# A hybrid mixer and MoE layer on one core: six 256-column slots of the first projection as seven block products each, with the convolution's channels among them

## The chip, the cores and the metric

The kernel is one program on one core of a Trainium2 chip. The metric is device time in microseconds, the median over runs. Engines: PE (TensorE, matmul), with its weight loads shown as PEld, DVE (VectorE), ACT (ScalarE), POOL (GpSimd), and SP (SyncE), which here only issues DMAs. All arithmetic on PE is float32: the profile shows every float32 matmul as two MATMUL records, so 16 records of 512 columns are 8 matmuls.

## The reference, cut to what matters

```python
h = layer_norm(x, ln_in_g, ln_in_b)                 # (1024 tokens, 1024 channels)
proj = h @ w_in                                     # 7432 columns
(a_q, a_k, a_v, b_q, b_f, b_i, b_g, c_z, c_xbc, c_dt,
 d_q, d_k, d_v, d_f, gate) = split(proj)            # 512 128 128 256 256 256 256 256 512 4
                                                    # 256 256 256 4 4096
ya = swa_sink_attention(a_q, a_k, a_v, ...)         # mixer A
yb = hgrn2_mixer(b_q, b_f, b_i, b_g, ...)           # mixer B, the linear mixer: forget gate
                                                    # f = lb + (1-lb)*sigmoid(b_f), then log, cumsum
yc = mamba2_mixer(c_z, c_xbc, c_dt, ...)            # mixer C, convolution over c_xbc
yd = forgetting_attention(d_q, d_k, d_v, d_f)       # mixer D
g = sigmoid(gate)
merged = g0*(ya@w_br_a) + g1*(yb@w_br_b) + g2*(yc@w_br_c) + g3*(yd@w_br_d)
h = layer_norm(ALPHA*h + merged @ w_out)
h = layer_norm(ALPHA*h + moe_ffn(h))                # 64 experts, top 6, and a shared one
```

## The kernel before, in words

The input projection is cut into slots: 256 columns of w_in (1 MB), loaded by SP into one of two SBUF buffers (`g.wslot`, slot n into buffer n % 2). load_slot(n) waits until PE has used slot n-2. A slot has units. A feature-major unit ("fm", L284) makes 128 channels for 512 tokens: 8 matmuls of 512 columns over the 1024 input channels. A token-major unit ("tm", L290) makes 256 channels for 2 x 128 tokens: 16 matmuls of 256 columns (136 for the slot of mixer A's values and the eight small row channels). Units alternate between PSUM banks 6 and 7; ACT copies each out with one or two activations (read_unit, L303).

Stage 1 (norm_in_and_project) loads and normalizes x, turns it with PE transposes into `g.hT` (channels on partitions) in two halves of 512 tokens, and projects slots 0 to 7: two of mixer A's queries, BF (forget gate), AK, the AV slot with the small rows, BQ, and BI and BG (mixer B's values and gates, tm). PE's own order is: transposes of the first half, units 0 and 1, transposes of the second half (L619), unit 2, a small table of biases (bias_rows, L628), then all the other units. Beside it POOL writes the rows of h to DRAM (L470, L472, DMA L474, eight times: the h_rows loop). ACT and DVE make the forget gate: Sigmoid (L522) once BF is out, scale (L585), key and floor (L589, L591), Ln (L528), two scans (L595).

Then one block holds mixers A, B, C and D, one after another on every engine. Each mixer's PE code calls fill(n) between its own steps, which issues n parts (an eighth of a unit) of the following slots: in mixer A those of CX (c_xbc, 512 channels in two slots, fm, destination `g.cX`), in B those of CZ, DQ, DK, DV and a gate slot, in C three gate slots. A gate unit is staged by ACT (L328) in one buffer that a DMA of SP spills to DRAM (L355) before the next may be staged.

In mixer D eleven gate slots are computed in the block form: the product of the weight slot (2 x 2 blocks of 512 input channels x 128 output channels) with hT (2 x 2 blocks of 512 x 512) is made from seven block products of 4 matmuls each (gate_part, L1566), instead of 32 matmuls. It needs four sums of hT's blocks (t1 to t4, DVE, L1649 to L1654), four sums of weight blocks in every slot (mix_weights, POOL, L1517 to L1522), and combinations of results: ACT copies products r = 0, 2, 4, 6 out of one bank (L1731), DVE adds or copies r = 1, 3, 5 from the other (L1670, L1666), POOL adds two of the results (L1539). A product is allowed when the one two before it has left its bank. In D's start PE waits for all units of mixer C to be read out (`pe.wait_ge(g.proj_read, g.first_unit[g.slots_d])`), does fill(8), that is products r = 0 and 1, and then waits for a row that comes by way of DVE (`drop`, L1656), SP's DMAs (L1495) and the semaphore drop_in, before its first scores (L1595).

After the mixers come the merge, output projection with routing, and the experts (L2840, L2856), whose weights (3 MB each) SP streams when PE has finished with a buffer.

## Time and profile before

| | us |
|---|---|
| median of 3 runs (2185.29 to 2189.09) | 2185.38 |
| the profiled execution, its own time | 2187.7 |
| its span, first to last instruction | 2185.9 |
| PE busy | 2091.0 (96%) |
| DVE, POOL, ACT busy | 1058.4, 666.8, 423.2 |
| mean granted TensorE clock | 0.985 |

Busy times of two engines overlap. Matmul durations of the profile contain the pipeline's length, so what a matmul costs in a stream is read from the distance of starts. The granted clock is 1.00 at 2.4 GHz and 0.50 at 1.2 GHz.

### The profile page before, as it was taken

Reading aid. Unit: us, or ns where it says so; the run is one execution under the profiler, and the core shown is the slowest. Engines: PE = TensorE matmul, PEld = TensorE weight load, DVE = VectorE, ACT = ScalarE, POOL = GpSimd, SP = SyncE. Lnnn points to the kernel's source line nnn. Section 1 sums busy time; section 2 is a strip of 40 time slices with the busy share of each in tenths; the row PEclk is TensorE's granted clock in tenths of the full one; section 3 lists DMA queues with packets and bytes.
Section 4 is the critical chain, followed back from the end, with each engine's and each line's share of the span. In section 5 each row is a group of like instructions: output and inputs, shape, how many; then the busy total and the mean of one; then the engine's idle time right before and its main releaser. Section 6 shows DMA issues by size and latency. Waiting matters only on the chain. (4 is left out here: it accounts for less than half of the span.)

```text
span 2185.9 us, 23006 instructions
## 1 busy us (share of the span) xinstructions
PE 2091.0 (96%) x7177; PEld 1102.2 (50%) x7178; DVE 1058.4 (48%) x2940; ACT 423.2 (19%) x909; POOL 666.8 (31%) x582
## 2 busy tenths in 40 slices
PE   7999999999999999999999999899999999999990
PEld 4458667574644455553444554344444444444440
DVE  4010455558561222221223755686666666666646
ACT  2020333334321111111221222011111111111112
POOL 0800002221132212112442001355545545555533
PEclk9999999999999999999999999999999999999995
DMA  5311001002122211116336004699999999999964
GB/s 144 131 49 39 20 20 32 27 20 68 44 68 77 77 54 62 54 63 226 106 96 222 34 35 163 229 336 348 350 353 359 358 360 354 350 349 355 350 200 155
DMA packets 129900, 368.24 MB, mean 168 GB/s; under 512 B 34332, under 2 KB 66192, under 8 KB 104352
## 3 DMA queue, kind: packets, MB, share of 16 engines
q1 hardware_dynamic: 104224, 312.64, 38.4%
q0 software_dynamic: 23520, 54.61, 10.4%
q8 instruction: 44, 0.72, 0.1%
q10 hardware_dynamic: 2080, 0.01, 0.1%
q14 instruction: 32, 0.26, 0.0%
HBM read 318.37 MB, written 68.16 MB: 177 GB/s over the span
## 5 line engine op out<-in xcount | busy, mean ns | idle before, releaser
L2840 PE MATMUL banks<-arena 128*128 128x512 f32 x1056 | 468.8, 597 | 3.0 <-DVE arena L2833 0.8
L284 PE MATMUL banks<-arena 128*128 128x512 f32 x864 | 397.3, 596 | 3.0 <-PEq L108 3.0
L2819 POOL DMA_INDIRECT arena<-h_rows,index x268 | 276.4, 1031 | 153.3 <-DVE index L2803 73.9
L2840 PEld LDWEIGHTS banks<-arena 128*128 128x128 f32 x1056 | 195.2, 190 | 225.8 <-issue 224.7
L1566 PE MATMUL banks<-arena 128*128 128x512 f32 x616 | 282.7, 601 | 3.1 <-ACT arena L328 3.1
L2856 PE MATMUL banks<-arena 128*128 128x512 f32 x528 | 237.6, 592 | 1.3 <-ACT arena L2655 0.8
L284 PEld LDWEIGHTS banks<-arena 128*128 128x128 f32 x864 | 157.7, 192 | 154.7 <-issue 144.7
L2833 DVE STREAM_TRANSPOSE arena<-arena 128x1024 f32<-128x1024 f32 x66 | 133.9, 2028 | 133.5 <-PE banks L2840 133.5
L2827 POOL DMA_INDIRECT sums<-arena,row_to x66 | 107.1, 1623 | 274.4 <-DMA sums<-arena,row_to 250.4
L1566 PEld LDWEIGHTS banks<-arena 128*128 128x128 f32 x616 | 111.6, 192 | 120.8 <-issue 115.8
L2856 PEld LDWEIGHTS banks<-arena 128*128 128x128 f32 x528 | 100.2, 190 | 127.0 <-issue 125.3
L2803 DVE TENSOR_SCALAR index<-row 32x1 uint32<-32x1 f32 x1072 | 155.4, 145 | 17.1
L1815 PE MATMUL banks<-arena 128*128 128x512 f32 x320 | 138.1, 593 | 1.6 <-DMA arena<-in_w_br_d_dram 1.6
L290 PE MATMUL banks<-arena 128*128 128x256 f32 (+1 forms) x640 | 129.6, 360 | 0.0
L1977 PE MATMUL banks<-arena 128*128 128x512 f32 x256 | 114.2, 600 | 4.2 <-PEq L1785 2.8
L290 PEld LDWEIGHTS banks<-arena 128*128 128x128 f32 x640 | 110.9, 190 | 13.5 <-issue 1.4
L2650 ACT ACTIVATE arena<-banks 128x256 f32<-128x256 f32 x65 | 24.9, 383 | 434.6 <-PE banks L2840 434.6
L1844 DVE TENSOR_TENSOR arena<-arena,banks 128x512 f32<-128x512 f32 x64 | 44.0, 688 | 129.9 <-PE banks L1815 98.6
L1815 PEld LDWEIGHTS banks<-arena 128*128 128x128 f32 x320 | 60.4, 190 | 78.9 <-issue 68.9
L793 DVE CUSTOM_DVE_ANT_0 arena<-banks,arena,sinks 128x192 f32<-128x192 f32 (+1 forms) x64 | 23.6, 406 | 127.9 <-PE banks L735 71.0
L2565 DVE TENSOR_SCALAR arena<-banks,weight 128x512 f32<-128x512 f32 x64 | 48.0, 750 | 75.7 <-PE banks L2856 75.7
L2662 ACT ACTIVATE arena<-banks,weight 128x512 f32<-128x512 f32 x64 | 44.0, 687 | 203.6 <-PE banks L2856 203.6
(376 smaller groups left out, 2254.3 us busy)
## 6 DMA issues: line engine op xcount, KB each, us to landing
arena<-in_w_exp_gate_dram SPq DMA_DIRECT2D x66, 1024.0 KB, 8.8
arena<-in_w_exp_up_dram SPq DMA_DIRECT2D x66, 1024.0 KB, 11.5
arena<-in_w_exp_down_dram SPq DMA_DIRECT2D x66, 1024.0 KB, 18.1
arena<-in_w_in_dram SPq DMA_DIRECT2D x26, 1024.0 KB, 5.3
gates<-arena SPq DMA_DIRECT2D x60, 256.0 KB, 2.0
arena<-gates SPq DMA_DIRECT2D x60, 256.0 KB, 2.6
arena<-h_rows,index POOLq DMA_INDIRECT x268, 3.0
arena<-in_x_dram SPq DMA_DIRECT2D x8, 512.0 KB, 5.9
```

What stands on the lines that cost most here:

```text
L284: mm = pe.matmul(bank[0:width], w[:, q, col:col + width], g.hT[:, q, at * HALF:(at + 1) * HALF], start=(q == 0), stop=(q == KT - 1))
L290: mm = pe.matmul(bank[:, m * width:(m + 1) * width], g.hT[:, k, (at + m) * P:(at + m + 1) * P], w[:, k, col:col + width], start=(k == 0), ...
L1566: mm = pe.matmul(gate_bank(n, b), left[:, k, :], right[:, k, :], start=(alone and k == 0), stop=(k == 3), skip_group_check=True)
L1815: mm = pe.matmul(bank[:, 4 + p % 2, :], wbr[:, k, j * P:(j + 1) * P], g.yT[:, k, h * HALF:(h + 1) * HALF], start=(k == tiles[b][0]), stop= ...
L1977: mm = pe.matmul(bank[:, h, :], merged[:, k, m * P:(m + 1) * P], wout[k][:, h * HALF:(h + 1) * HALF], start=(k == 0), stop=(k == KT - 1))
L2565: dve.tensor_scalar(w.y[c % 2][:, HALF:], bank[:, 5, :], g.weight[:, c % 4:c % 4 + 1], None, ALU.mult).then_inc(s["yb"], 1)
L2803: ins = dve.tensor_scalar(g.index[32 * b:32 * b + 32, k, q:q + 1], g.row[32 * q:32 * q + 32, k, :], 4.0, float(b), ALU.mult, ALU.add)
L2819: return pool.indirect_dma_start(w.x[k][:, 256 * q:256 * (q + 1)], None, rows, bass.IndirectOffsetOnAxis(ap=g.index[:, k, q:q + 1], axis=0 ...
L2827: return pool.indirect_dma_start(g.sums, bass.IndirectOffsetOnAxis(ap=g.row_to[:, b:b + 1], axis=0), w.y[k], None, bounds_check=last, oob_ ...
L2833: return dve.transpose(w.xT.rearrange("p k (q n) -> p q k n", q=4), w.x[k].rearrange("p (q n k) -> p q k n", q=4, k=KT))
L2840: mm = pe.matmul(g.bank[:, 2, :].rearrange("p (a f) -> p a f", a=2), xT[:, k, :], wgu[:, :, k, :], start=(k == 0), stop=(k == KT - 1))
L2856: mm = pe.matmul(g.bank[:, 4 + h, :], hidT[:, k, :], wdn[:, k, h * HALF:(h + 1) * HALF], start=(k == 0), stop=(k == 1))
```

## The change

Six slots of stage 1 (BF, the two of mixer A's queries, BQ, and both CX) are made in the block form, 28 matmuls instead of 32, with results written straight to their destinations. Their products use the same banks 6 and 7, and the same split over ACT, DVE and POOL. Slots 0 and 1 are now AK (one piece) and AV with the small rows (three pieces); their six units come first in the order key, value, value, key, value, value, so that three units precede the transposes of the second half. BI and BG leave stage 1 and become the fill of mixer A in place of CX. The sums t1 to t4 are made on DVE after the second half of hT is there, t3 a second time later into another place. POOL gets the weight sums and the crossing adds between its h_rows steps. Semaphores of the block form are shared with mixer D, whose counts start at six slots. D's first product waits for one unit fewer, its second for the last.

```diff
+    keys = [(0, unit) for unit in fm(halves(g.kA, HD))]
+    values = [(1, unit) for unit in tm(values_and_rows, 0, P + 8, 2)]
+    slot([(0, AK, P)], [keys[0], values[0], values[1], keys[1]])
+    slot([(0, AV, P), (P, CDT, 4), (P + 4, DF, 4)], values[2:])
+    g.rows_unit = sum(len(x.units) for x in S)
+    g.blocks_from = len(S)
+    slot(whole(BF), [])            # and two of AQ, BQ, two of CX: no units
...
+    g.slots_a = len(S)
     slot(whole(BI), tm(wide(g.igB, 0), 0, 256, 2))
     slot(whole(BG), tm(wide(g.igB, 256), 0, 256, 2))
-    g.slots_a = len(S)
-    for c in range(2):
-        slot(whole(CX + 256 * c), fm(...cX...) + fm(...cX..., P))
     g.slots_b = len(S)
@@ SP, stage 1
             load_slot(g, sp, 0)
+            load_slot(g, sp, 1)
             (x tiles 4 to 7, small parameters)
-            load_slot(g, sp, 1)
+            load_slot(g, sp, 2)
...
-            for n in range(2, g.slots_a + 2):
+            for n in range(3, g.slots_a + 2):
+                if 0 <= n - 2 - g.blocks_from < N:
+                    sp.wait_ge(prod, 7 * (n - 1 - g.blocks_from))
                 load_slot(g, sp, n)
@@ POOL, stage 1
+            def mix_weights(n):            # four tensor_tensor of 128x512, as in mixer D
+            def cross(n):
+                pool.wait_ge(copied, 4 * n + 3)
+                pool.wait_ge(joined, 3 * n + 2)
+                pool.tensor_tensor(kept(n, 4), kept(n, 4), kept(n, 3), ALU.add).then_inc(crossed, 1)
+            mix_weights(0)
+            mix_weights(1)
+            keep_row(0); keep_row(1); cross(0); keep_row(2); keep_row(3); mix_weights(2)
+            keep_row(4); cross(1); keep_row(5); keep_row(6); mix_weights(3); keep_row(7)
+            cross(2); mix_weights(4); (clears); cross(3); mix_weights(5); ...; cross(4); cross(5)
@@ ACT, stage 1
+            for n in range(N):
+                for r in range(0, 7, 2):
+                    act.wait_ge(prod, 7 * n + r + 1)
+                    if r == 6:
+                        act.wait_ge(crossed, n + 1)
+                    act.activation(kept(n, r), block_bank(n, 0), ACT.Copy).then_inc(copied, 1)
+                    (n == 3, r == 0: Ln)
+                (n == 0: Sigmoid, when copied >= 4, joined >= 3, crossed >= 1)
@@ DVE, stage 1
+            t1, t3, t2, t4 after turned(1)
+            join(0); forget gate scale; rows copy; join(1); join(2); key; floor; t3_late
+            join(3); scans; join(4); join(5)
@@ PE, stage 1
+            def block_part(n, r):          # 4 matmuls of 128x512
+                if r == 0: waits for the slot's load and joined >= 3n
+                elif r == 1: copied >= 4n
+                elif r % 2: joined >= 3n + r // 2
+                else: copied >= 4n + r // 2
+                if r == 2: wsum >= 4n + 4, tsum >= 4 (5 from n = 4)
@@ PE, mixer D
-                if n:
-                    pe.wait_ge(s["joined"], 3 * n)
+                pe.wait_ge(*((s["joined"], 3 * (first + n)) if n else (g.proj_read, g.first_unit[g.slots_d] - 1)))
             elif r == 1:
-                if n:
-                    pe.wait_ge(s["copied"], 4 * n)
+                pe.wait_ge(*((s["copied"], 4 * (first + n)) if n else (g.proj_read, g.first_unit[g.slots_d])))
...
-        pe.wait_ge(g.proj_read, g.first_unit[g.slots_d])
         fill(8, "start")
```

## Rows read from the trace of the kernel before

**Rows 1.** Stages: time, busy PE, PEld, DVE, ACT, POOL (instructions), granted clock, DMA share, GB/s.

```profile
47.15:222.75 175.60, 175.58 (x633) 110.12 (x632) 10.34 (x11) 24.61 (x39) 45.43 (x30) 0.99 0.23 77
222.75:344.70 121.95, 120.19 (x593) 79.31 (x594) 57.72 (x224) 41.11 (x153) 3.78 (x2) 1.00 0.08 27
...
1460.00:2080.00 620.00, 615.94 (x1901) 291.75 (x1900) 406.85 (x1401) 75.24 (x168) 312.87 (x276) 1.00 1.00 354
```

**Rows 2.** SP's waits over the whole span: total us, times, longest.

```profile
SPq L2353 <- PE banks L2856: 585.3, 61, 17.3
```

**Rows 3.** PE in order of time, stage 1: start us, us, what.

```profile
32.66 3.66 PE L619 MATMUL banks<-ident,arena 128*128 128x128 f32 x32
...
43.12 4.11 PE L628 MATMUL banks<-arena 32*128 32x256 f32 x16
47.16 77.15 PE L284 MATMUL banks<-arena 128*128 128x512 f32 x176
124.14 14.99 PE L290 MATMUL banks<-arena 128*128 128x136 f32 x128
...
167.31 55.42 PE L290 MATMUL banks<-arena 128*128 128x256 f32 x256
```

**Rows 4.** Groups of mixer D's block form: busy us, mean ns, idle before.

```profile
L1731 ACT ACTIVATE arena<-banks 128x512 f32<-128x512 f32 x44 | 26.2, 595 | 139.8 <-PE banks L1566 137.4 <-DMA gates<-arena 2.4
...
L1670 DVE TENSOR_TENSOR arena<-arena,banks 128x512 f32<-128x512 f32 x22 | 15.1, 686 | 48.9 <-PE banks L1566 48.9
L1520 POOL TENSOR_TENSOR arena<-arena 128x512 f32<-128x512 f32 x11 | 14.1, 1283 | 0.0
```

**Rows 5.** Mixer B, steps of L1075 with tm fill between, then with fm fill.

```profile
356.87 1.47 PE L1075 MATMUL banks<-arena 128*16 128x32 f32 x16
...
366.20 1.47 PE L1075 MATMUL banks<-arena 128*16 128x32 f32 x16
...
384.85 1.47 PE L1075 MATMUL banks<-arena 128*16 128x32 f32 x16
...
394.15 1.47 PE L1075 MATMUL banks<-arena 128*16 128x32 f32 x16
```

**Rows 6.** POOL in order of time: two consecutive h_rows transfers.

```profile
70.25 0.58 POOL L474 DMA_DIRECT2D h_rows<-arena  x1 [0.31 <-POOL arena L472]
...
75.93 0.57 POOL L474 DMA_DIRECT2D h_rows<-arena  x1 [0.30 <-POOL arena L472]
```

**Rows 7.** ACT in order of time: the forget gate's Sigmoid.

```profile
111.22 1.28 ACT L522 ACT_TABLE_LOAD   x1
112.52 1.91 ACT L522 ACTIVATE arena<-arena 128x2048 f32<-128x2048 f32 x1
```

**Rows 8.** DVE in order of time: statistics of x tiles 4 to 7.

```profile
20.53 4.83 DVE L537 BATCH_NORM_STATS2 stats<-arena 128x6 f32<-128x512 f32 x8
```

**Rows 9.** The stretch in which the AV slot's three pieces are loaded (columns as in rows 1).

```profile
111.80:115.00 3.20, 3.20 (x9) 1.42 (x8) 0.00 (x0) 2.61 (x2) 0.00 (x0) 1.00 0.96 169
```

**Rows 10.** All engines in order of time where mixer D starts.

```profile
634.35 0.60 ACT L328 ACTIVATE arena<-banks 128x512 f32<-128x512 f32 x1
...
637.77 10.12 PE L1566 MATMUL banks<-arena 128*128 128x512 f32 x16 [3.12 <-ACT arena L328]
...
646.78 1.26 POOL L1517 TENSOR_TENSOR arena<-arena 128x512 f32<-128x512 f32 x1 [2.11 <-DMA arena<-arena]
...
647.73 0.39 PE L1595 MATMUL banks<-arena 128*128 128x128 f32 x2
```

**Rows 11.** Three stretches and their granted clock (columns as in rows 1).

```profile
46.50:49.90 3.40, 3.40 (x6) 1.21 (x6) 0.00 (x0) 0.79 (x2) 0.00 (x0) 0.50 0.37 154
...
637.77:643.80 6.03, 6.03 (x7) 2.52 (x8) 5.16 (x2) 0.00 (x0) 5.86 (x4) 0.50 0.70 217
...
990.11:993.13 3.02, 0.00 (x0) 0.03 (x1) 0.00 (x0) 0.78 (x2) 0.00 (x0) 1.00 0.24 90
```

More of the change, by code:

```diff
@@ L390, in norm_in_and_project, with weights, sums, block_bank @@
     ones_rows = g.region(YT0 + 8192, T)
+    N = len(g.block_out)
+    half = slice(0, 4), slice(4, 8)
+    tok = [[g.hT[:, k, h * HALF:(h + 1) * HALF] for h in range(2)] for k in half]
+    t1, t2 = g.region(R2 + 4096, 4, HALF), g.region(R2 + 6144, 4, HALF)
+    t3, t4 = g.region(R3 + 2056, 4, HALF), g.region(R3 + 4 * (T + 3), 4, HALF)
+    t3_late = g.region(YT0, 4, HALF)
+    mixed = [[g.region(a, 4, P) for a in at] for at in (
+        (R3, R3 + 512, R3 + 1024), (R3 + 1536, WK + 4608, R1 + 7296),
+        (YT0 + 2048, YT0 + 2560, YT0 + 3072), (YT0 + 3584, YT0 + 4096, YT0 + 4608))]
+    g.block_sems = {n: sem("k_" + n) for n in "tsum wsum prod copied joined crossed".split()}
+    tsum, wsum, prod, copied, joined, crossed = (g.block_sems[n] for n in "tsum wsum prod copied joined crossed".split())
+    def weights(n):
+        w = g.wslot[(g.blocks_from + n) % 2]
+        return [[w[:, k, i * P:(i + 1) * P] for k in half] for i in range(2)]
+    def sums(n):
+        return mixed[n % 2 if n < 4 else 2 + n % 2]
+    def block_bank(n, b):
+        return bank[:, 6 + (n + b) % 2, :]
+    def kept(n, r):
+        a, b = g.block_out[n]
+        place = {0: (a, 0), 1: (a, 0), 2: (a, 1), 5: (a, 1), 4: (b, 1), 3: (b, 0), 6: (b, 0)}[r]
+        return place[0][:, place[1] * HALF:(place[1] + 1) * HALF]
+    def loaded(eng, n):
+        eng.wait_ge(g.w_loaded[(g.blocks_from + n) % 2], slot_bytes(g, g.blocks_from + n))
     def row(a):
@@ L466, in _, with keep_row @@
             pool.wait_ge(rel_ready, 4)
-            for m in range(NT):
+            def keep_row(m):
                 if m >= 2:
@@ L474, in _ @@
                 pool.dma_start(g.h_rows[m * P:(m + 1) * P, :], h_row[m % 2]).then_inc(h_kept[m % 2], 16)
+            keep_row(0)
+            keep_row(1)
+            cross(0)
+            keep_row(2)
+            keep_row(3)
+            mix_weights(2)
+            keep_row(4)
+            cross(1)
+            keep_row(5)
+            keep_row(6)
+            mix_weights(3)
+            keep_row(7)
+            cross(2)
+            mix_weights(4)
             for k in range(2):
@@ L479, in _ @@
             pool.memset(ones_rows[:, 0:T:P], 0.0).then_inc(cleared, 1)
+            cross(3)
+            mix_weights(5)
             for b in range(2):
@@ L586, in _ @@
                                   ALU.mult, ALU.add).then_inc(gate, 1)
+            dve.wait_ge(rows_turned, 1)
+            dve.tensor_copy(g.rows[:].rearrange("p (b n) -> p b n", b=2), bank[0:8, 0:2, :]).then_inc(rows_read, 1)
+            join(1)
+            join(2)
             dve.wait_ge(gate, 2)
@@ L596, in _ @@
                                        ALU.mult, ALU.add).then_inc(scanned, 1)
+            for n in range(4, N):
+                join(n)
             dve.wait_ge(scanned, 2)
-            dve.wait_ge(rows_turned, 1)
-            dve.tensor_copy(g.rows[:].rearrange("p (b n) -> p b n", b=2), bank[0:8, 0:2, :]).then_inc(rows_read, 1)
             dve.wait_ge(rows_read, 1)
@@ L633, in _ @@
             pe.wait_ge(g.const_ready, 4)
+            def block_part(n, r):
+                (a11, a12), (a21, a22) = weights(n)
+                s1, s2, s4 = sums(n)
+                third = t3 if n < 4 else t3_late
+                left, right, b, alone = ((a11, tok[0][0], 0, True), (a12, tok[1][0], 1, True), (s2, t2, 0, False),
+                                         (s1, t1, 1, True), (a21, third, 0, False), (s4, tok[1][1], 1, False),
+                                         (a22, t4, 0, False))[r]
+                if r == 0:
+                    loaded(pe, n)
+                    pe.wait_ge(*((joined, 3 * n) if n else (g.proj_read, g.rows_unit - 1)))
+                elif r == 1:
+                    pe.wait_ge(*((copied, 4 * n) if n else (g.proj_read, g.rows_unit)))
+                elif r % 2:
+                    pe.wait_ge(joined, 3 * n + r // 2)
+                else:
+                    pe.wait_ge(copied, 4 * n + r // 2)
+                if r == 2:
+                    pe.wait_ge(wsum, 4 * n + 4)
+                    pe.wait_ge(tsum, 4 if n < 4 else 5)
+                for k in range(4):
+                    mm = pe.matmul(block_bank(n, b), left[:, k, :], right[:, k, :], start=(alone and k == 0),
+                                   stop=(k == 3), skip_group_check=True)
+                mm.then_inc(prod, 1)
             turn_tiles()
@@ L1725, in copy @@
                 if r % 2 == 0:
-                    act.wait_ge(s["prod"], x + 1)
+                    act.wait_ge(s["prod"], 7 * first + x + 1)
                     if r == 0:
```

150 lines of the change are left out of this document (97 added, 53 removed).

## The prediction

> **What bounds the kernel now.** I read the busy time by stage first. In stage 1 PE is busy 175.58 of 175.60 us, in mixer A 120.19 of 121.95, and both run at full clock but for a short stretch [rows 1]. In the experts PE is busy 616 of 620 us while the DMA engines are at a share of 1.00 and 354 GB/s [rows 1], so there two resources are full. Next I read SP's waits: for an expert's weights it waits for PE 61 times, 585 us in all [rows 2]. So the stream is released by PE and moves with it; time taken from stage 1 should arrive at the end unless something later has its own clock. Then I read PE in order of time through stage 1: it goes from one unit to the next without a gap [rows 3], so what counts there is the number of matmuls, and any new wait in which PE stands. Last I read the start of mixer D, because the change touches PE's waits there.
>
> **What a matmul costs.** From 47.16 to 124.14 PE issues 176 records, which is 11 fm units [rows 3]. Until 49.90 the clock is at half [rows 11], so 2.74 us of it gave half the work, 1.37 lost. (76.98 - 1.37)/11 = 6.87 us for a unit of 8 matmuls, 0.859 for a matmul. A tm unit of 256 columns costs (55.42 less the last one's tail of about 0.17)/8 = 6.91, one of 136 columns 14.82/4 = 3.71 [rows 3].
>
> **The block form in stage 1.** Six slots go from 32 to 28 matmuls: 24 x 0.859 = **20.6 us less**, if the products follow each other without a wait. A product (4 matmuls) lasts 3.44 us. Its bank is needed again two products later, so one whole product, 3.44 us, covers the reading: 0.60 us on ACT or 0.69 on DVE [rows 4]. The matmuls are the same form as mixer D's, so no loss at the seams is charged.
>
> **The order at the beginning.** The first half of hT feeds AK's first unit and two value units: 6.87 + 2 x 3.71 = 14.3 us where two fm units took 13.7. The transposes (32.66 before) start at 33.2; unit 3 ends at 33.2 + 10.5 = 43.7 (32.66 to 43.12 before), bias_rows at 47.7 (43.12 to 47.16), the last two value units with the half-clock stretch behind bias_rows at about 56.6 [rows 3, 11]. That is only another order of the same units, price nothing. The AV slot with its 16-byte pieces is now loaded ahead of x's second half. The row says that the whole slot takes 3.2 us of nearly full DMA engines at 169 GB/s [rows 9]; AK adds half a megabyte, and both replace a slot of 1 MB in four pieces. DVE's statistics of tiles 4 to 7 began with no wait for a DMA [rows 8], and PE takes those tiles only at 32.66. I charge nothing. The Trainium skill (DMA: Bandwidth & Descriptors, Specifications) puts line rate at 512 B and more for a piece and a read-modify-write below that; by that rule the slot would be dear ahead of x, and the row's 169 GB/s agrees in kind, but the slot is through in 3.2 us all the same.
>
> **What POOL must bring in time.** A weight sum or crossing takes 1.28 us [rows 4], a slot's four sums about 5.3 with the handovers; an h_rows step takes 75.93 - 70.25 = 5.7 us [rows 6]. Slot 3 is asked for at 56.6 and I let it land at 63.5 (four pieces; an estimate, twice the 3.2 of rows 9). mix_weights(1) ends near 69, two h_rows steps near 80.1, cross(0) near 81.4. PE runs slot 0's products from 56.6 to 80.6. The seventh product's copy waits for the crossing and ends at 82.0; Sigmoid with its table takes 3.2 us on ACT [rows 7], until 85.2; then the next slot's first product, ready at 84.9, is copied by 85.8. PE needs that copy at 88.4 (third product of slot 1). So the tightest place has 2.6 us to spare. Later ones have more: I reckon cross(1) at 103.8 to 105.1 against the seventh product at 105.5, cross(2) at 128.8 against 129.5, weight sums 14 us or more ahead. Behind the waiting ACT stand only the next slot's copies, behind POOL's wait the next h_rows steps, which nobody needs before DVE's key. The price of the scheme is **0**; without that cover each us beyond 2.6 costs one.
>
> **The tail of the forget gate.** Ln is put behind slot 3's first copy, the scans behind slot 3's last join. They take the gaps of a product each: 1.28 + 1.91 on ACT [rows 7] fits into the 6.87 between two of its copies; the scans are followed by a join 10 us later. **0**.
>
> **BI and BG into mixer A.** Stage 1 loses 8 tm units and gets none of CX's fm ones there (they are in the six slots): 8 x 0.04 = 0.3 less. Mixer A gets them: 64 parts, tm for fm. Mixer B shows the same exchange between the same steps: 9.33 us with tm fill against 9.30 with fm, 8 parts each [rows 5], so 64 parts cost **0.2 to 0.3**. Together with the 0.3 it is nothing.
>
> **Mixer D's start.** Before, PE waits 3.12 us until ACT has staged C's last unit, and then runs 16 records in 10.1 us where 6.87 would do [rows 10], for the clock was at half from 637.77 to 643.80 [rows 11]. After, the first product waits only for the second last unit, staged at 634.95 [rows 10]. So PE starts 2.8 us earlier and keeps its clock: products 0 and 1 end near 641.8. But then it waits for drop_in. POOL waits for the same semaphore and goes on at 646.78 [rows 10]; nothing of that path (DVE's sums, its row, four DMAs) changes. So PE stands for 5 us, and the scores start at 646.8 instead of 647.7: 0.9 gained. What follows the wait is the question. An idle stretch of 3.12 us brought half clock (6.03 us, 3.0 lost), one of 3.02 us at 990.11 did not, and the stretch behind bias_rows was 3.4 us (1.7 lost) [rows 10, 11]. A wait of 5 us is longer than both, so I take a fall, this time in front of the scores, where mixer D is bound by PE: 1.7 to 3.0 lost, middle 2.3. In sum **+1.4** (0.8 to 2.1; -0.9 with no fall). The Trainium skill (TensorE: Matmul & The Clock Gate, HAM oscillation) says that PE bursts between long waits each begin at half clock; by it the fall is certain, by rows 11 alone it is likely.
>
> **Sum** against the profiled execution: 2187.7 - 20.6 - 0.3 + 0.3 + 1.4 = 2168.5. That execution was 2.3 above the median of the runs shown (2185.38), so the forecast for the median is 2168.5 - 2.3 = **2166.2 us**.
>
> **Rivals.**
> - *The clock does not fall in D.* For it: the 3.02 us that left the clock at full [rows 11]; against it: the wait is longer by 2 us. 2185.4 - 20.6 - 0.9 = 2163.9. Chance 0.12.
> - *POOL is late.* The h_rows steps and the slot loads are serial on POOL, ACT's seventh copy waits for the crossing, and Sigmoid stands in front of the next slot's copies. If POOL's order runs 3 to 10 us later than reckoned at the first crossing, PE stands for what exceeds 2.6: 2167 to 2174. Against it: all its prices are of this trace. Chance 0.07.
> - *Slower: a wait at every product.* If the copy of a product does not fit into the next product, PE stands at each of 42 seams. It decides from (19.2 + 4.4)/42 = 0.56 us each on; at 1 us each the time is 2185.4 - 19.2 + 42 = 2208. For it: ACT and DVE must be free at the moment, and both have other work of 1 to 3 us in stage 1 [rows 7]; against it: a cover of 3.44 us for 0.6 to 0.69 [rows 4], ACT busy 25 and DVE 10 of 176 us [rows 1]. Chance 0.03.
> - *The change gives nothing at the end.* The experts have the DMA engines full [rows 1]; if their stream had a start of its own, the 20 us would be waited off there: 2185.4. Against it: rows 2. Chance 0.03.
>
> **How the numbers follow.** My forecast has 0.75, with a range of its own of 2163.5 to 2169 (D's bounds, 1 us of POOL, and the runs' own spread). The range for 8 in 10 takes in the rival with no fall and half of the late POOL: 2161 to 2172. 0.2% of the time, 4.4 us, is about what a measurement of this kernel can tell from no change. Faster by more: 0.75 + 0.12 + 0.07 = 0.94, less 0.01 for a very late POOL, 0.93. Within it: 0.03 and 0.01, 0.04. Slower: 0.03.
>
> **What would show it.** Stage 1's PE ends about 21 us earlier (near 201.6), with 168 block matmuls and no idle time ahead of them; ACT's copies have no long wait for POOL; cross(0) starts after two h_rows steps, near 80. Mixer A lasts 120 to 122 us. In D PE idles 4 to 5 us between products 1 and the first scores, and half clock follows. It is wrong if block matmuls in stage 1 show idle time on ACT or DVE, if x's second half comes later than 33 us, or if the experts' stage gets longer.

## The result, and the profile after

The changed kernel takes 2176.84 us, median of 6 runs (2170.03 to 2179.06), beside 2186.49 (2183.95 to 2189.11, 6 runs) before: a ratio of 0.9947 [0.9933, 0.9962]. The forecast, 2166.2 against 2185.38, was a ratio of 0.9912. The direction is right, the size is not: about 10 us came instead of 19 (11.6 by the ratio, which is not that of the two medians and is the figure that carries the interval). The changed kernel was timed against the one before twice more (below), at 0.9932 [0.9919, 0.9946] and 0.9931 [0.9917, 0.9944], some 15 us.

The profiled execution took 2170.03 us with a span of 2168.3. It is the lowest of its six, so its trace is read for places and durations, and totals are read from several executions.

The stretches of the changed kernel, columns as in [rows 1]; they answer to stage 1, the experts and the half-clock stretches of [rows 11]:

```profile
47.15:205.00 157.85, 155.37 (x409) 72.13 (x408) 28.74 (x30) 23.29 (x35) 83.70 (x61) 0.99 0.28 87
...
90.69:92.86 2.17, 0.01 (x1) 0.00 (x1) 2.12 (x3) 0.60 (x1) 2.17 (x1) 1.00 0.00 0
93.50:96.90 3.40, 3.40 (x6) 1.44 (x5) 0.00 (x0) 0.00 (x0) 3.21 (x4) 0.54 0.41 159
624.40:628.70 4.30, 0.06 (x1) 0.02 (x1) 1.04 (x2) 0.00 (x0) 0.00 (x0) 1.00 0.18 59
629.40:632.80 3.40, 3.40 (x5) 1.22 (x4) 0.31 (x2) 0.46 (x2) 3.24 (x4) 0.54 0.00 0
1440.00:2060.00 620.00, 615.87 (x1902) 291.62 (x1901) 408.54 (x1402) 75.40 (x168) 315.47 (x277) 1.00 1.01 353
```

PE is idle 2.5 us in stage 1 where it was never idle. The first row and that of before end at different distances from mixer A's first record, so the gain in stage 1 is read from that record: 205.63 for 223.66, 18.0 us earlier. Two pairs stand out: 2.17 us in which PE does nothing, then 3.4 us at half clock; and 4.3 us without PE in front of D's scores, then again 3.4 us at half clock. The experts' row agrees with that of before (PE busy 615.87 for 615.94 us).

PE in order of time through stage 1 (start, us, what), beside [rows 3]:

```profile
43.40 3.96 PE L741 MATMUL banks<-arena 32*128 32x256 f32 x16
47.29 7.68 PE L291 MATMUL banks<-arena 128*128 128x136 f32 x64
54.81 24.20 PE L767 MATMUL banks<-arena 128*128 128x512 f32 x56
78.84 1.04 PE L792 MATMUL banks<-ident,tok_rows 128*8 128x128 f32 x8
79.72 10.98 PE L767 MATMUL banks<-arena 128*128 128x512 f32 x24
92.86 111.83 PE L767 MATMUL banks<-arena 128*128 128x512 f32 x256 [2.17 <-DVE arena L682]
205.63 0.56 PE L876 MATMUL banks<-arena 128*128 128x384 f32 x1 [0.94 <-PEq L436]
```

336 records are the forecast's 168 matmuls, 56 records in 24.20 us the forecast's 24.0. The value units take 7.68 us: the clock did not fall behind bias_rows here, so PE stands 1.8 us earlier at 54.81 than the 56.6 of the forecast. Mixer A starts at 205.6, not at 202.5.

PE's wait for DVE's line 682 is in the bracket above. PE's waits at D's start (what waits, what it waits for, us in total, times, longest): a new one for a DMA, and what is left of the 3.12 us for ACT in [rows 10]:

```profile
PE banks L1737 <- DMA arena<-arena: 4.2, 1, 4.2
...
PE banks L1709 <- ACT arena L329: 0.4, 1, 0.4
```

**What DVE does while PE stands at L682's join.** A join is DVE's adding of product 1, 3 or 5 of a slot into its destination (product 3 is only copied); it frees the bank for the product two later. The crossing is POOL's adding of two results. Line 692 holds the forget gate's two scales, 695 the copy of the token rows, 682 the second slot's first join. DVE in order of time:

```profile
86.49 4.59 DVE L692 TENSOR_SCALAR arena<-arena,oml,lb 128x1024 f32<-128x1024 f32 x2 [10.19 <-ACT arena L613]
91.01 1.21 DVE L695 COPY rows<-banks 8x1024 f32<-8x1024 f32 x1
92.14 0.67 DVE L682 TENSOR_TENSOR arena<-arena,banks 128x512 f32<-128x512 f32 x1
```

ACT at the same place, lines 605 (copies of products) and 613 (Sigmoid):

```profile
82.64 0.60 ACT L605 ACTIVATE arena<-banks 128x512 f32<-128x512 f32 x1 [9.86 <-POOL arena L513]
83.25 1.28 ACT L613 ACT_TABLE_LOAD   x1
84.55 1.91 ACT L613 ACTIVATE arena<-arena 128x2048 f32<-128x2048 f32 x1
86.36 0.58 ACT L605 ACTIVATE arena<-banks 128x512 f32<-128x512 f32 x1
```

POOL (513 is the crossing, 525 and 527 the h_rows steps):

```profile
81.26 1.28 POOL L513 TENSOR_TENSOR arena<-arena 128x512 f32<-128x512 f32 x1
82.50 2.34 POOL L525 TENSOR_TENSOR arena<-arena 128x1024 f32<-128x1024 f32 x1
84.91 2.36 POOL L527 TENSOR_TENSOR arena<-arena 128x1024 f32<-128x1024 f32 x1
...
88.17 2.36 POOL L525 TENSOR_TENSOR arena<-arena 128x1024 f32<-128x1024 f32 x1
90.60 2.69 POOL L527 TENSOR_TENSOR arena<-arena 128x1024 f32<-128x1024 f32 x1
```

The crossing starts at 81.26 (forecast 80.1), ACT's copy of the seventh product ends at 83.2 (82.0), Sigmoid at 86.46 (85.2), slot 1's first copy at 86.9 (85.8). That is the forecast's chain, 1.1 to 1.3 us late, while PE is 1.8 us early: of 2.6 us of slack none is left, and the 24 records in front of the wait take 10.98 us where 10.46 would do. Behind this lies the larger thing. DVE waits for Sigmoid, and then its scales and the copy of rows, 5.65 us, stand between it and a join that PE's next product needs.

**The start of mixer D**, engines in order of time, beside [rows 10]:

```profile
616.62 0.60 ACT L329 ACTIVATE arena<-banks 128x512 f32<-128x512 f32 x1
...
617.36 7.11 PE L1709 MATMUL banks<-arena 128*128 128x512 f32 x16 [0.43 <-ACT arena L329]
...
623.14 1.71 DVE L1798 TENSOR_SCALAR arena<-rows 8x1024 f32<-8x1024 f32 x1
...
624.93 2.52 SPq L1640 DMA_DIRECT2D arena<-arena  x4
...
628.71 0.46 PE L1737 MATMUL banks<-arena 128*128 128x128 f32 x2 [4.25 <-DMA arena<-arena]
...
629.06 8.78 PE L1709 MATMUL banks<-arena 128*128 128x512 f32 x16
```

This is the forecast's picture: the first two products at full clock (7.11 us for 16 records where [rows 10] had 10.12), 4.25 us of waiting for the drop's DMAs, then 16 records in 8.78 us at half clock.

**Stage lengths over several traces.** The traced executions of one kernel differ by 5.5 and 7.1 us, so stages are compared as means, worked out from the start of each stage's first PE record, over four traces of before (2187.70, 2190.52, 2187.59, 2185.01 us) and six of the changed kernel (2170.03, 2170.58, 2174.61, 2171.48, 2168.82, 2175.88):

| stage, mean us | before | changed | difference | forecast |
|---|---|---|---|---|
| until mixer A | 223.1 | 205.1 | -18.0 | -20.9 |
| mixer A until B | 133.2 | 133.5 | +0.3 | +0.3 |
| B until D's first scores | 289.9 | 289.6 | -0.3 | -0.9 |
| D's scores until the merge | 361.0 | 363.3 | +2.3 | +2.3 |
| merge until the output projection's first record | 154.4 | 154.5 | +0.1 | 0 |
| output projection until the experts' last product with the gate and up weights | 965.8 | 965.9 | +0.1 | 0 |
| all, with what follows | 2187.7 | 2171.9 | -15.8 | -19.2 |

Of the 3.4 us between the last two columns 2.9 lie ahead of mixer A and 0.6 ahead of D's first scores; the other rows nearly cancel. The last stage holds the output projection, the routing and the experts.

### The profile page after: what moved, and what is told of

It is laid out like the page before. It is cut to its first block and busy times, and to the rows that moved or that the text cites. A ratio compares the mean times of both kernels' runs of the same rounds, so it can differ in the third digit from the quotient of the medians.

```text
span 2168.3 us, 23007 instructions
## 1 busy us (share of the span) xinstructions
PE 2068.5 (95%) x7129; PEld 1091.5 (50%) x7130; DVE 1085.7 (50%) x2963; ACT 423.7 (20%) x909; POOL 704.1 (32%) x612
## 5 line engine op out<-in xcount | busy, mean ns | idle before, releaser
L2982 PE MATMUL banks<-arena 128*128 128x512 f32 x1056 | 470.0, 598 | 3.0 <-DVE arena L2975 0.8
L2982 PEld LDWEIGHTS banks<-arena 128*128 128x128 f32 x1056 | 195.7, 190 | 226.6 <-issue 225.4
L1709 PE MATMUL banks<-arena 128*128 128x512 f32 x616 | 281.4, 599 | 0.4 <-ACT arena L329 0.4
L2998 PE MATMUL banks<-arena 128*128 128x512 f32 x528 | 237.6, 592 | 1.3 <-ACT arena L2797 0.8
L285 PE MATMUL banks<-arena 128*128 128x512 f32 x480 | 220.2, 596 | 3.0 <-PEq L108 3.0
L1709 PEld LDWEIGHTS banks<-arena 128*128 128x128 f32 x616 | 111.1, 191 | 117.3 <-issue 116.2
L2998 PEld LDWEIGHTS banks<-arena 128*128 128x128 f32 x528 | 100.2, 190 | 127.0 <-issue 125.3
L767 PE MATMUL banks<-arena 128*128 128x512 f32 x336 | 147.0, 599 | 2.2 <-DVE arena L682 2.2
L1957 PE MATMUL banks<-arena 128*128 128x512 f32 x320 | 138.4, 593 | 1.8 <-DMA arena<-in_w_br_d_dram 1.8
L291 PE MATMUL banks<-arena 128*128 128x256 f32 (+1 forms) x640 | 139.9, 360 | 0.0
L285 PEld LDWEIGHTS banks<-arena 128*128 128x128 f32 x480 | 86.7, 191 | 83.9 <-issue 82.7
L291 PEld LDWEIGHTS banks<-arena 128*128 128x128 f32 x640 | 108.6, 191 | 18.6 <-issue 1.3
L2119 PE MATMUL banks<-arena 128*128 128x512 f32 x256 | 112.9, 594 | 5.0 <-PEq L1927 3.0
L767 PEld LDWEIGHTS banks<-arena 128*128 128x128 f32 x336 | 64.0, 192 | 83.7 <-issue 79.1
L1957 PEld LDWEIGHTS banks<-arena 128*128 128x128 f32 x320 | 60.4, 190 | 79.5 <-issue 69.1
```

Of the source, the lines that this page charges most:

```text
L285: mm = pe.matmul(bank[0:width], w[:, q, col:col + width], g.hT[:, q, at * HALF:(at + 1) * HALF], start=(q == 0), stop=(q == KT - 1))
L291: mm = pe.matmul(bank[:, m * width:(m + 1) * width], g.hT[:, k, (at + m) * P:(at + m + 1) * P], w[:, k, col:col + width], start=(k == 0), ...
L767: mm = pe.matmul(block_bank(n, b), left[:, k, :], right[:, k, :], start=(alone and k == 0), stop=(k == 3), skip_group_check=True)
L1709: mm = pe.matmul(gate_bank(n, b), left[:, k, :], right[:, k, :], start=(alone and k == 0), stop=(k == 3), skip_group_check=True)
L1957: mm = pe.matmul(bank[:, 4 + p % 2, :], wbr[:, k, j * P:(j + 1) * P], g.yT[:, k, h * HALF:(h + 1) * HALF], start=(k == tiles[b][0]), stop= ...
L2119: mm = pe.matmul(bank[:, h, :], merged[:, k, m * P:(m + 1) * P], wout[k][:, h * HALF:(h + 1) * HALF], start=(k == 0), stop=(k == KT - 1))
```

## The experiments

**same_again**: the changed kernel without an edit, on the chip of the next three.

> The changed kernel unchanged, for the spread of its runs and a second trace. Its profiled execution (2170.0) was the fastest of six, the others lay at 2173 to 2179. Theory 1 (clock): the same instructions meet the clock at another phase, so slower executions show more stretches at half clock, in stage 1, at the start of mixer D or behind the waits of the later stages; each is worth 1.5 to 3.5 us; the stage lengths agree otherwise within 0.3 us. Theory 2 (DMA): the slower executions have longer expert stages at full clock, with PE waiting for weights. Median 2173 to 2179 in both.

2171.37 us (2169.78 to 2176.03) beside 2188.39 for before: 0.9932 [0.9919, 0.9946], which is 14.9 us by the ratio and 17.0 between the medians. The expected 2173 to 2179 did not come back. So part of the first result's distance to the forecast was of its executions, not of the kernel. The traced execution (2170.58) is again one of the shorter ones, so it decides between neither theory; it has mixer A at 205.5 all the same.

**scale_later**: DVE's scales and the copy of rows go behind the second slot's first join.

```
 joins, slot 1, product 1:  first join
+                           if n == 1: scale_gate()
-dve.wait_ge(sig, 1)
-for j in range(2): dve.tensor_scalar(g.fB[:, j, :], ...)
-dve.wait_ge(rows_turned, 1)
-dve.tensor_copy(g.rows[:]..., bank[0:8, 0:2, :])
+def scale_gate(): (the same five lines)
```

> DVE scales the forget gate behind the first join of the second slot instead of ahead of it. Theory of the seam: DVE's two scales take 4.6 us there because POOL's h_rows operations run beside them (1.5 us before the change), and with the copy of the rows they hold up the join on which PE stands for 2.2 us, after which the clock falls for 3.4 us (1.7 lost). Behind the join they have 6.9 us until the next one. PE's idle time ahead of the second slot's fourth product goes from 2.2 to 0, stage 1 ends 2 to 4 us earlier, the time falls by 2 to 4 us. Rival: the scales only move the wait to the next join: no gain.

2173.49 us (2167.74 to 2174.8), 0.9926 [0.9913, 0.994]. The join now comes first and PE runs its 280 records in one piece; mixer A starts at 204.4 because this execution had half clock behind bias_rows (10.08 us for the value units, 2.4 more than in the trace above). DVE, POOL and PE of this kernel, in order of time:

```profile
90.19 0.69 DVE L682 TENSOR_TENSOR arena<-arena,banks 128x512 f32<-128x512 f32 x1 [10.49 <-PE banks L771]
90.79 3.89 DVE L694 TENSOR_SCALAR arena<-arena,oml,lb 128x1024 f32<-128x1024 f32 x2
```
```profile
89.00 2.36 POOL L525 TENSOR_TENSOR arena<-arena 128x1024 f32<-128x1024 f32 x1
91.44 2.69 POOL L527 TENSOR_TENSOR arena<-arena 128x1024 f32<-128x1024 f32 x1
```
```profile
48.29 10.08 PE L291 MATMUL banks<-arena 128*128 128x136 f32 x64
...
83.12 120.33 PE L771 MATMUL banks<-arena 128*128 128x512 f32 x280
```

The wait was DVE's order, as thought, and the scales are slow here too, beside POOL's two instructions. The trace has no stall between products at all: from the record behind the transposes until mixer A it is 121.3 us (204.39 - 83.12), where the changed kernel has 125.9 (205.63 - 79.72). The time does not show it: the median lies 2.1 us above same_again's, where 2 to 4 less was forecast, and the intervals overlap.

**pool_waits**: the scales stay, POOL is silent while they run, and does that h_rows work later.

```
 crossing 0
+pool.wait_ge(gate, 2)          # both scales done
 keep_row(2), keep_row(3)
-keep_row(4)
 mix weights, crossing 1
+keep_row(4)
...
-keep_row(7)                    # the same behind crossing 2
-dve.tensor_tensor(t3_late, ...)   # in front of join(3)
+dve.tensor_tensor(t3_late, ...)   # behind it
```

> POOL waits with its third h_rows step until DVE's two scales are done, the crossings of slots 2 and 3 stand ahead of the h_rows steps that they followed, and the late third sum of tokens is made behind slot 4's joins. Port theory: with POOL silent the two scales take 1.5 us instead of 4.6, DVE's join is in time and PE does not wait at it (2.2 us less, and the fall of the clock behind it). Rival: the scales are slow for another reason (they still take over 4 us), or POOL's h_rows chain, 5 us later, makes ACT's seventh copies or DVE's key late, and PE waits 1 to 4 us there instead.

2169.78 us (2164.78 to 2171.03, 4 runs), 0.9909 [0.9894, 0.9925]. DVE, POOL and PE of this kernel:

```profile
86.18 1.53 DVE L693 TENSOR_SCALAR arena<-arena,oml,lb 128x1024 f32<-128x1024 f32 x2 [10.24 <-ACT arena L614]
88.77 0.67 DVE L683 TENSOR_TENSOR arena<-arena,banks 128x512 f32<-128x512 f32 x1
```
```profile
80.96 1.28 POOL L513 TENSOR_TENSOR arena<-arena 128x512 f32<-128x512 f32 x1
87.79 2.35 POOL L525 TENSOR_TENSOR arena<-arena 128x1024 f32<-128x1024 f32 x1 [5.56 <-DVE arena L693]
```
```profile
79.36 121.10 PE L768 MATMUL banks<-arena 128*128 128x512 f32 x280
201.40 0.88 PE L877 MATMUL banks<-arena 128*128 128x384 f32 x2 [0.94 <-PEq L436]
```

The same two scales take 1.53 us instead of 4.59 (one by one 0.81 and 0.81 for 1.34 and 3.34; the kernel before has 0.81 each, with POOL idle beside them). The second of the slow pair ends at 91.1, just behind the POOL instruction that ends at 90.53. The join comes at 88.8 instead of 92.1, PE does not stand at it, and mixer A starts at 201.4. From the record behind the transposes until mixer A it is 122.0 us (201.40 - 79.36) where the changed kernel has 125.9. Of these 3.9 us 1.7 are half clock (111.83 us for 256 records where the trace after_look1, below, has 110.13) and 2.2 standing. It is not the whole price of the scheme: this kernel still needs 0.8 us more than scale_later's 121.3, for its 280 records take 121.10 us where 120.33 would do, in short stalls of 0.2 to 0.3 us between products. Most of them are the late chain on ACT, of which the changed kernel has 0.5. Against scale_later the changed kernel loses 4.6 us. The medians, 1.6 us below same_again's with overlapping intervals, can't show either figure.

**d_waits_for_all**: D's first product waits for every staged unit again; one line.

```
-(g.proj_read, g.first_unit[g.slots_d] - 1)
+(g.proj_read, g.first_unit[g.slots_d])
```

> In mixer D the first product waits again for all of mixer C's units; all else as in the changed kernel. Theory: PE idles 3 us there, is slowed in its first two products, and then has no wait of 4.2 us ahead of the first scores, so that mixer D's scores start about 1 us later but at full clock. The time is 1 to 2.5 us shorter than with the early start when the clock falls before the scores, 1 us longer when it does not. Rival: the early start is worth what it moves, 3 us: the time is 2 to 4 us longer.

2171.39 us (2169.23 to 2171.86), 0.9921 [0.9908, 0.9935], beside 2171.37 for same_again. PE's waits in it hold this one in place of the two of the changed kernel:

```profile
PE banks L1709 <- ACT arena L329: 3.2, 1, 3.2
```

Its scores start 1.1 us later (290.7 us after B instead of 289.6), its D takes 361.1 instead of 363.3. By the trace that is 1.1 us to the good, which its timing can't show.

**row_first**: DVE makes the drop's row ahead of the two sums t2 and t4, so that its four DMAs go out earlier.

```
+dve.wait_ge(g.c_yT_read, NT)
+dve.tensor_scalar(drop, g.rows[:], -8.0, None, ALU.mult)
 t2, t4
-(the same two lines)
```

> In mixer D DVE makes the row of decay values ahead of the second and fourth sum of tokens instead of behind them; all else as in the changed kernel. Theory: PE's wait of 4.2 us ahead of D's first scores is the row's lateness (DVE's sums, then four DMAs). With the row 6 us earlier SP's own last spill of mixer C is what is late next, so the wait shrinks to 0 to 1.5 us and the clock does not fall behind it: 3 to 6 us less, median near 2167 to 2170. Rival: the sums, now later, are missing at the third product, and PE waits 2 to 4 us there instead: no gain.

2167.3 us (2164.99 to 2171.4, 6 runs) beside 2186.77 for before, 0.9911 [0.9894, 0.9927]; this is another chip than that of the changed kernel's own timings. The start of D in it:

```profile
615.37 2.37 DVE L1794 TENSOR_SCALAR arena<-rows 8x1024 f32<-8x1024 f32 x1
...
620.62 2.52 SPq L1640 DMA_DIRECT2D arena<-arena  x4
...
624.98 0.46 PE L1737 MATMUL banks<-arena 128*128 128x128 f32 x2 [2.07 <-DMA arena<-arena]
```

and the stretch behind the wait:

```profile
625.00:632.00 7.00, 7.00 (x19) 3.40 (x20) 0.45 (x2) 1.06 (x3) 4.99 (x4) 1.00 0.03 11
```

The wait is 2.07 us instead of 4.25 and the clock stays full. The scores start 287.4 us after B and not 289.6; D takes 361.5 and not 363.3. That is 4.0 us in the trace for two moved lines. The median is where the theory had it (the wait is not: 0 to 1.5 us were expected), but the interval reaches into those of the changed kernel.

**products_doubled**: on pool_waits, the second product of each of the six slots is computed twice into its bank, with the same result: 24 matmuls more, as many as the change removes.

```
-for k in range(4):
+for k in (range(4) if r != 1 else (0, 1, 2, 3, 0, 1, 2, 3)):
```

> As the kernel in which POOL waits for DVE's scales (2169.8, 0.9909 of before), with the second block product of each of the six slots computed twice into the same bank, the second time over the first: 24 matmuls more, as many as the block form saved. Theory: a matmul is worth 0.859 us here and arrives whole at the end: 20.6 us more, 2189 to 2192, about the time of before. Rival: the experts' stream of weights has a pace of its own and absorbs a part: clearly less than 20.6 us, under 2185.

2190.84 us (2186.86 to 2194.43, 12 runs), 1.0015 [1.0005, 1.0024]: 21.1 us above pool_waits' 2169.78 (two chips; by the ratios 0.0106 x 2186.8 = 23.2, with an error of some 4). Forecast for 24 matmuls: 20.6. Mixer A starts at 222.4 instead of 201.4, and from the output projection to the experts' last it is 970.4 us beside 966.5. The closest pair is this trace and that of pool_waits_row_first (below): stage 1 differs in the 24 matmuls alone, neither has a stall between products, and both have the same half clock behind bias_rows. From the start of bias_rows until mixer A they take 179.9 and 159.3 us: 20.6. Nothing downstream absorbs time given in stage 1.

**before_early_d**: the kernel before, with the change's early start of D and nothing else.

```
-pe.wait_ge(g.proj_read, g.first_unit[g.slots_d])      # ahead of all products
+(g.proj_read, g.first_unit[g.slots_d] - 1)            # product 0
+(g.proj_read, g.first_unit[g.slots_d])                # product 1
```

> The kernel before with mixer D's early start alone: the first product waits for one unit fewer. Theory: the 3.1 us wait there disappears, a wait of 4 to 5 us for the row appears ahead of the scores, with the clock falling behind it: 0 to 2 us longer than before. Rival: the early start is a gain by itself: 1 to 3 us shorter.

2192.77 us (2186.18 to 2197.31, 12 runs) beside 2186.77 (23 runs): 1.0022 [1.001, 1.0035], 4.8 us slower by the ratio and 6.0 between the medians. PE's wait in it:

```profile
PE banks L1592 <- DMA arena<-arena: 4.6, 1, 4.6
```

So the early start costs by itself, as forecast in sign (0 to 2 us were expected). But the size is two to three times that of the traces (2.1 us, below), and the 12 runs are no single cloud: three stand at 2186 with a mean granted clock of 0.986 to 0.987, nine at 2190 to 2197 with 0.981 to 0.985.

**early_look1, early_look2**: two more traces of before_early_d, for where its time goes; **after_look1, after_look2**: two of the changed kernel beside them.

> The kernel before with mixer D's early start, one more profiled execution. Its twelve executions fall into two heaps, three at 2186 and nine at 2190 to 2197, and the one traced was of the lower heap. Theory: in the upper heap the wait of 4.6 us ahead of D's first scores is followed by a longer or second stretch at half clock, 6.8 to 13.7 us in mixer D where the lower one has less, so that D from its first scores to the merge lasts 365 to 370 us instead of 363. Rival: the extra time is in stages that the edit does not touch (behind bias_rows in stage 1, or from the output projection on).

> As the look before it, for a third execution: the same two theories, by the length of each stage and its stretches at half clock.

> The changed kernel, a third profiled execution. The two traced (2170.0, 2170.6) were of its faster ones; most others lay at 2173 to 2179. Theory: a slower one shows 3 to 8 us more, all of it in stretches at half clock behind bias_rows, behind the join in stage 1 or behind the wait in mixer D. Rival: in later stages.

> As the look before it, for a fourth execution of the changed kernel: the same two theories.

before_early_d: 2189.25 and 2188.64 (before beside them 2187.84). In its three traces B until scores is 290.0, 289.6 and 289.6, D 363.3, 364.0 and 362.6: +2.1 us in sum against before. None of the three is one of the executions above 2190, so what those hold was not seen.

The changed kernel: 2174.61 and 2171.48. The first of them had the half clock behind bias_rows, and is the counter-check on the forecast's slack. PE in it:

```profile
46.91 9.35 PE L291 MATMUL banks<-arena 128*128 128x136 f32 x64
...
81.01 10.46 PE L767 MATMUL banks<-arena 128*128 128x512 f32 x24
92.35 110.13 PE L767 MATMUL banks<-arena 128*128 128x512 f32 x256 [0.88 <-DVE arena L682]
```

PE comes 1.3 us later to the place, the 24 records take their 10.46 us, the wait shrinks to 0.88, the clock does not fall behind it (110.13 us for the 256 records), and mixer A starts at 203.4, *earlier* than in the executions without the first fall. A PE that is delayed by its clock loses less at the join.

This execution, and that of changed_timed (2175.88, below), are the longest of the traced. The theory placed the extra time in the three places that the forecast knew, the rival in later stages, and it is mostly the rival: from the output projection on they take 968.7 and 969.9 us beside 963.8 in the profiled execution, with 17 us of that stage at half clock in each (8.5 lost) where the profiled one has 3.4 (1.7 lost). after_look1 has besides 2.1 us more in D (365.0 for 362.9).

**before_look1 to before_look3, after_look3**: three more traces of the kernel before, for the mean of its stages, and one of the changed kernel on the same chip.

> The kernel before, a second profiled execution. From the output projection's first matmul to the experts' last, four executions with the old stage 1 (one of them the kernel before) took 963.9 to 965.8 us, mean 964.6, ten with the new one 963.8 to 970.4, mean 966.5, with the same instructions. Theory of chance: it is where the stretches at half clock happen to lie, and more executions of the kernel before reach 966 to 969 too. Rival: the change moves the later stages, and the kernel before stays at 963.5 to 966. Stage 1 ends at 220 to 224 by whether the clock falls behind bias_rows.

> As the look before it, a third execution of the kernel before: later stages 964 to 969 by chance, 963.5 to 966 by the rival.

> As the look before it, a fourth execution of the kernel before: later stages 964 to 969 by chance, 963.5 to 966 by the rival. Mixer D from its first scores to the merge 361 in all of them, since the stretch at half clock lies ahead of the scores.

> The changed kernel, a fifth execution: D from its first scores to the merge 362.5 to 365, against 361 before; first matmul of mixer A at 203 to 206; later stages 964 to 969.

2190.52, 2187.59, 2185.01 and 2168.82 (before beside them 2182.19). The stages are in the table above. PE of the third, beside [rows 3]:

```profile
41.91 3.80 PE L628 MATMUL banks<-arena 32*128 32x256 f32 x16
45.64 75.80 PE L284 MATMUL banks<-arena 128*128 128x512 f32 x176
...
220.80 0.88 PE L735 MATMUL banks<-arena 128*128 128x384 f32 x2 [0.94 <-PEq L404]
```

bias_rows takes 3.80 us and the 176 records 75.80, where [rows 3] have 4.11 and 77.15: in this execution the clock never fell there, and mixer A starts 2.9 us earlier. It also gives a price of the change: from the start of bias_rows until mixer A it is 178.9 us (220.80 - 41.91), and 158.4 in pool_waits (201.40 less 43.04), neither with half clock, the second with its 0.8 us of short stalls. Without these the difference is 21.3: 20.5 for the 24 matmuls, 0.3 for BI and BG, and 0.5 that the new order of the units only moves ahead of bias_rows (14.3 us of units for 13.7). The changed kernel has 162.2 there in five of its six traces. The stage from the output projection on ranges from 964.4 to 967.9 in before and from 962.8 to 969.9 in the changed kernel, with means of 965.8 and 965.9, so what one pair of traces shows there is chance. One of the three added traces of before goes above 966, as that theory wants; after_look3's 962.8 is below the 964 that was expected.

The same execution waits 3.11 us for ACT in front of D's first product, as the profiled one does (3.12), and keeps full clock; then it waits 1.55 us for the drop. In all three added traces of before the scores start 289.6 us after B, as in the changed kernel; only the profiled one, slowed for 6.8 us in its first two products, has 290.9.

**pool_waits_row_first, combined_timed**: both mended orders together, timed on two chips; **changed_timed**: the changed kernel on the second of them.

> POOL silent beside DVE's scales, and the row first in mixer D: both edits. If the seam in stage 1 and the wait in mixer D are two separate stalls, the gains add: 4 to 5 us for the first and 3 to 6 for the second against the changed kernel, median 2162 to 2166. Rival: what one gives, the clock takes elsewhere: no better than either alone (2168 to 2170).

> POOL silent beside DVE's scales and the row first in mixer D, timed again beside the changed kernel. Expected 3 to 8 us below it, 0.989 to 0.991 of before. If both stalls were only chance of the clock, the two are within 2 us.

> The changed kernel timed again, beside the combined version on one chip. The ratios so far are 0.9947 and 0.9932 to before; what the traces of five executions give is 2171.1/2187.7 = 0.9924. Expected 0.992 to 0.995, median 2170 to 2176.

2166.58 us (2165.76 to 2168.31) beside 2186.77 for before, 0.9904 [0.9888, 0.992]; and on the other chip 2170.03 (2169.02 to 2171.16) beside 2187.97, 0.9916 [0.9903, 0.993]. The changed kernel there: 2172.91 (2172.07 to 2175.88), 0.9931 [0.9917, 0.9944]. Its lowest run is above the highest of the combination, the medians lie 2.9 us apart: the only gain of the mends that the times themselves show. In the traces the combination has mixer A at 201.9 and 202.1 and the scores 287.5 us after B. Its 0.9904 is the lowest ratio of all, though pool_waits' 0.9909 and row_first's 0.9911 lie within its interval. The two mends give less than the 3.9 and 4.0 us of their traces, and less than the 2162 to 2166 and the 3 to 8 us that were expected: half clock still follows the wait for the drop in both traces (D 363.1 and 364.3, not row_first's 361.5), though that wait is now 2.23 and 2.17 us. For pool_waits_row_first, the first scores and the stretch behind them (columns as in [rows 1]):

```profile
622.93 0.46 PE L1738 MATMUL banks<-arena 128*128 128x128 f32 x2 [2.23 <-DMA arena<-arena]
```
```profile
623.80:627.20 3.40, 3.40 (x6) 1.34 (x5) 0.15 (x1) 0.46 (x2) 3.24 (x4) 0.50 0.00 0
```

## Why the prediction was wrong in size, and where it was right

**24 matmuls, 20.6 us: right.** 56 records take 24.20 us, 24 matmuls put back into stage 1 lengthen it by 20.6 us (179.9 for 159.3) and the whole by 21.1 to 23.2, and behind bias_rows the change without any stall saves 21.3, of which 0.3 are the tm units and 0.5 is only moved.

**The order at the beginning, nothing: about right.** The transposes of the second half start at 32.6 to 32.9 in the changed kernel's traces and at 31.2 to 31.5 in three of the four of before; only the profiled execution, on which the forecast stood, had them at 32.66 [rows 3]. Of the 1.1 us between the means 0.5 is the moved work (14.3 us of units for 13.7), which comes back behind bias_rows; the forecast was right to drop it. The other 0.6 is that PE's first unit starts at 18.2 to 18.6 and not at 17.3 to 17.6. The profiled execution of before has 18.61 as well and pool_waits_row_first 17.75, so it may be chance; that the AV slot ahead of x's second half causes it is neither shown nor excluded.

**BI and BG into mixer A, +0.3: right**, 133.5 against 133.2.

**Mixer D's start, +1.4: right in mechanism and size.** A wait of 4.25 us (forecast 4 to 5), the clock at half behind it, +2.3 us in D. The scores gain 0.3 us and not 0.9, so the sum is +2.0, the upper end of 0.8 to 2.1. The 0.9 was read from the one execution of before whose first two products ran at half clock for longest; in the other three the scores came no later than in the changed kernel. d_waits_for_all, which undoes it in the changed kernel, gives 1.1 us back in its trace and nothing that its median shows; before_early_d puts it at 4.8 by its ratio. Which of these sizes holds in the executions that were not traced stays open.

**No stream of its own in the experts: right.** The rival that absorbs the gain falls with products_doubled, that of a wait at every product with the single pieces of 56, 256 and 280 records.

**The failed step: "The price of the scheme is 0", with "The tail of the forget gate ... 0".** The forecast followed ACT up to slot 1's first copy and gave it 2.6 us of slack. It never put DVE's own work in front of the second slot's join: two scales, which must wait for Sigmoid (86.46), and the copy of rows. With POOL silent they take 1.53 + 1.21 us, and the join comes at 88.8, in time (pool_waits, no wait at it). Beside POOL's h_rows steps the scales take 4.59 us, the join starts at 92.14, PE stands 2.17 us, and then 3.4 us pass at a granted clock of 0.54. That is 2.2 + 1.7 = 3.9 us, as much as pool_waits takes away. Another 0.5 us is the slack itself that was mis-sized: the chain to slot 1's first copy came 1.1 us late, PE 1.8 us early, and 2.6 us did not cover both. Against scale_later, which has no stall, the term forecast at 0 measures 4.6 us in five traces of six. In its effect it is the rival "POOL is late" (PE stands for what exceeds the slack), but not in its cause: POOL's crossing was 1.2 us late and not 3 to 10, and what POOL did beside DVE was the larger trouble. The Trainium skill (SBUF — State Buffer, Who interferes with whom) says that a copy or tensor_scalar of DVE in its two-port mode and a GpSimd instruction hold one shared pair of ports in turn, the other being blocked for the whole of an instruction; the traces agree, 1.53 us alone against 4.59 and 3.89 beside POOL. They show that it is POOL's work beside DVE that makes the scales slow; that the cause is the ports is the page's reading and was not tested. The question that the forecast left out is which engine runs beside each DVE instruction that a join waits for.

**The rest of the distance.** By traces the changed kernel is 15.8 us faster, the forecast said 19.2. Ahead of mixer A: -20.9 for the matmuls and tm units; +4.0 for the failed step (4.6 in five traces, 1.1 in after_look1); +0.6 for the later start of the first unit; and -1.8, because half clock behind bias_rows cost before 1.7, 3.4, 3.4 and 0 us in its four traces, 2.1 in the mean, and the changed kernel once 1.7, 0.3 in the mean. That makes, to 0.1, the -18.0 of the table. So the failed step was larger than the shortfall, and part of it was hidden by luck of the clock. The base was low too: 2185.38 was the median of three runs, later medians of before were 2186.5 to 2188.4. What no trace explains in full is the first result itself: five of its six executions took 2173.1 to 2179.1 us, while 11 of the 13 later ones took under 2175.5. Their mean granted clocks were 0.981 to 0.984 against 0.987 for the profiled one, and the two longest executions that were traced lost most in stretches at half clock from the output projection on (after_look1). But the clock is not all: in same_again 2169.78 and 2176.03 us both stand at 0.984.

## What to carry to other kernels

A slack is only as good as the list of what stands in the queue: for each join that PE waits for, write down everything its engine does before it, including work of another part of the kernel, and which engine runs beside it. DVE work on the critical path should not share its moment with long POOL work; keeping POOL silent for some 6 us cost nothing that the trace shows and gave back 3.9 in it. And an early start that ends in a longer wait further on is no gain: make the thing waited for earlier (row_first, two lines, 4.0 us in the trace) and not only the start. And read a term from more than one trace: the 0.9 us at D's scores stood in an execution of before that three others do not repeat.

## What the runs showed of the hardware

- Two DVE tensor_scalar of 128x1024 f32 take 1.53 us with POOL silent, 3.89 and 4.59 us beside POOL's tensor_tensor of 128x1024. POOL's own go from 2.35 to 2.69 us at the most.
- The same program does or doesn't drop to half clock at the same place: behind bias_rows, with PE busy throughout, 3 of 4 traces of before did and 1 lost nothing. At the join a wait of 2.17 us brought half clock in the profiled changed kernel, waits of 1.55 us (row_first) and 0.88 us (after_look1) did not. In D waits of 4.25, 2.23 and 2.17 us brought it (the last two in the combination) and one of 2.07 us (row_first) did not. The same wait of 3.1 us for ACT at D's start was followed by half clock in the profiled kernel before and not in before_look3.
- Executions of one kernel on one chip can differ as their mean granted clock does: before_early_d took 2186.2 us at 0.986 and 2197.3 at 0.981. 0.005 of 2190 us is 11 us, the whole difference. In same_again two executions 6.3 us apart have the same 0.984.
